# A stick-breaking attention stage: the sample pairs' value products moved behind the next pair's keys

## What is computed

```python
z = jnp.einsum('bqhd,bkhd->bhqk', qb, kb) * scale
log_beta = jnp.where(strict, jax.nn.log_sigmoid(z), NEG)
log_keep = jnp.where(strict, jax.nn.log_sigmoid(-z), 0.0)
later = lax.cumsum(log_keep, axis=3, reverse=True) - log_keep
w = jnp.exp(log_beta + later)
outs.append(jnp.einsum('bhqk,bkhd->bqhd', w, vb))
```

## Time and profile before

| | us |
|---|---|
| median of 3 runs | 1983.08 |
| lowest, highest | 1980.93, 1986.69 |
| the profiled execution | 1981.68 |
| its span | 1979.9 |
| the stage that is changed, first matmul to last copy-out | 1240.8 to 1382.2 of the span |

### The profile page before, as it was taken

How to read it: one execution, slowest core, us unless ns; L and a number is a source line. 1 busy time by engine, 2 the same in 40 slices (tenths; PEclk the granted TensorE clock), 3 DMA queues, 4 the chain that set the end, 5 groups by cost and what they waited for, 6 DMA issues and landing times.

```text
span 1979.9 us, 34330 instructions
## 1 busy us (share of the span) xinstructions
PE 1826.6 (92%) x13384; PEld 1635.6 (83%) x13384; DVE 1125.9 (57%) x2364; ACT 727.1 (37%) x1312; POOL 35.8 (2%) x65
## 2 busy tenths in 40 slices
PE   6999898989999799999999798787989999979997
PEld 5788456989999799987499796344989999979987
DVE  7973566467777642164232395675558777652263
ACT  5323345543323332245132223565553233242252
POOL 1300000000000000000000000000000000000000
PEclk9999788999999999999999857899999999989999
DMA  4134577212222232131122400864313222132211
GB/s 173 65 67 150 209 260 276 65 54 88 83 85 74 70 105 87 58 101 43 64 86 86 137 19 16 296 239 144 111 39 97 85 81 78 51 128 75 84 46 48
DMA packets 77948, 204.13 MB, mean 103 GB/s; under 512 B 12530, under 2 KB 14882, under 8 KB 77314
## 3 DMA queue, kind: packets, MB, share of 16 engines
q1 hardware_dynamic: 75762, 190.36, 28.8%
q0 software_dynamic: 2064, 12.06, 1.7%
HBM read 190.81 MB, written 10.40 MB: 102 GB/s over the span
## 4 chain that ended last, share of the span: by engine, by line
PE 79%; DVE 12%; SPq 3%; ACT 3%; issue 2%; DMA 1%; DVEq 0%; ACTq 0%
PE psum L400 42%; PE psum L573 12%; PE psum L1605 6%; PE psum L2148 3%; PE psum L408 2%; SPq L1300 1%; PE psum L832 1%; PE psum L1342 1%; PE psum L1317 1%; PE psum L495 1%; PE psum L2289 1%; PE psum L509 1%; DVE sb_arena_r L360 1%; DVE sb_ring_r L360 1%; SPq L1284 1%
## 5 line engine op out<-in xcount | busy, mean ns | idle before, releaser
L400 PE MATMUL psum<-sb_a_sb_r,sb_ring_r 128*128 128x288 f32 x1408 | 297.5, 295 | 0.0
L400 PE MATMUL psum<-sb_a_sb_r,sb_arena_r 128*128 128x288 f32 x1344 | 276.6, 296 | 0.0
L400 PE MATMUL psum<-sb_y_sb_r,sb_ring_r 128*128 128x288 f32 x960 | 263.5, 299 | 0.5 <-DVE sb_ring_r L360 0.5
L400 PEld LDWEIGHTS psum<-sb_a_sb_r,sb_ring_r 128*128 128x128 f32 x1408 | 231.3, 188 | 0.4
L400 PEld LDWEIGHTS psum<-sb_a_sb_r,sb_arena_r 128*128 128x128 f32 x1344 | 217.2, 188 | 0.0
L400 PE MATMUL psum<-sb_y_sb_r,sb_arena_r 128*128 128x288 f32 x704 | 207.2, 294 | 6.0 <-DVE sb_a_sb_r L360 5.9
L360 DVE TENSOR_TENSOR sb_ring_r<-sb_ring,sb_ring_r 128x1024 fp32r<-128x1024 f32 (+1 forms) x86 | 111.4, 1299 | 173.8 <-ACT sb_ring_r L357 172.9
L357 ACT ACTIVATE sb_ring_r<-sb_ring 128x1024 fp32r<-128x1024 f32 (+1 forms) x86 | 95.7, 1117 | 309.0 <-PE psum L400 249.1
L400 PEld LDWEIGHTS psum<-sb_y_sb_r,sb_ring_r 128*128 128x128 f32 x960 | 175.6, 190 | 1.5 <-DVE sb_ring_r L360 1.0
L573 PE MATMUL psum<-sb_arena_r 128*128 128x288 f32 x960 | 161.7, 304 | 8.2 <-DVE sb_arena_r L360 8.2
L400 PE MATMUL psum<-sb_arena_r,sb_ring_r 128*128 128x288 f32 x1056 | 145.9, 299 | 20.9 <-DVE sb_arena_r L360 20.9
(11 more groups left out here) (401 smaller groups left out, 3186.4 us busy)
## 6 DMA issues: line engine op xcount, KB each, us to landing
sb_ring<-w SPq DMA_DIRECT2D x166, 512.0 KB, 3.6
sb_ring<-wd SPq DMA_DIRECT2D x32, 704.0 KB, 4.1
sb_arena<-sb_v SPq DMA_DIRECT2D x64, 256.0 KB, 5.3
sb_arena<-moba_v SPq DMA_DIRECT2D x56, 256.0 KB, 6.6
sb_ring<-moba_k SPq DMA_DIRECT2D x32, 256.0 KB, 4.0
sb_a_sb<-moba_k SPq DMA_DIRECT2D x32, 256.0 KB, 5.5
sb_ring<-sb_k SPq DMA_DIRECT2D x32, 256.0 KB, 4.2
sb_a_sb<-sb_k SPq DMA_DIRECT2D x32, 256.0 KB, 5.2
```

Source lines behind the costliest of these rows:

```text
L400: ins = e.eng.matmul(out[:, half, :], fr(w[p][:, k, :]), fr(x[q][:, k, cols]), start=(first and k == 0 and i == 0), stop=(last and k == kb ...
```

## The change

The due lists of this stage get a third part, `final`, that holds for the last pair only. For pairs 0 to 2 the value products come behind units 12 and 13 (of the pair's own count) and the output transposes behind 16. The next pair's keys come behind unit 11. The scan keeps its place for pairs 0 to 2. For the last pair the values come behind unit 10, and log, softplus and scan one unit earlier than before.

Because the products of pair i now follow the keys of pair i+1, and both write bank 7, the waits change. In layer 1, from pair 1 on, PE waits before the keys until ACT has copied the pair before's transposed weights (`wt_ready`); the wait for its output (`y_copied`) moves from the new keys' scores to the transposes; and before its value products PE waits until DVE has read the next pair's new scores (`new_read`, a new semaphore, raised by L2662). Layer 0 keeps its due lists and waits.

```diff
         def between(pieces, u, last, due):
-            apart, units = due
+            apart, units, final = due
             for x in range(u, 8 * NPAIR + 16) if u == last else [u]:
                 for i, p in enumerate(pieces):
-                    for d in units:
+                    for d in units if i < NPAIR - 1 else final:
                         if apart * i + d == x:
                             next(p, None)
...
+            if layer == 1 and i >= 1:
+                pe.wait_ge(wt_ready, n)
             for s in range(2):
                 pe.wait_ge(kv_in[s], 16 * NPG * (n + 1))
...
                     if n >= 1:
-                        pe.wait_ge(y_copied, n)
+                        pe.wait_ge(y_copied, n if layer == 0 or i == 0 else n - 1)
...
             pe.wait_ge(sw_ready, n + 1)
+            if layer == 1 and i >= 1:
+                pe.wait_ge(y_copied, n)
             for g in range(NPG):
...
             pe.wait_ge(wt_ready, n + 1)
+            if layer == 1 and i + 1 < NPAIR:
+                pe.wait_ge(new_read, i + 2)
             for s in range(2):
...
-        DUE_A = {"pe": (8, (1, 2, 6, 7, 8, 9)), "act": (8, (5, 5, 6)), "dve": (8, (3, 4, 5, 9, 9))}
+        DUE_A = {"pe": (8, *[(1, 2, 6, 7, 8, 9)] * 2), "act": (8, *[(5, 5, 6)] * 2), "dve": (8, *[(3, 4, 5, 9, 9)] * 2)}
...
-        DUE_C = {"pe": (8, (2, 3, 9, 9, 9, 10)), "act": (8, (4, 5, 6, 8, 9)), "dve": (8, (4, 6, 7, 8, 10, 10))}
+        DUE_C = {"pe": (8, (3, 3, 10, 12, 13, 16), (3, 3, 9, 10, 10, 11)), "act": (8, (4, 6, 6, 9, 10), (4, 5, 5, 8, 9)),
+                 "dve": (8, (4, 6, 7, 8, 15, 17), (4, 5, 6, 8, 10, 11))}
...
-            do(stt(z[:, PAST:KEYS], s_new, ATT_SCALE, new, ALU.mult, ALU.add))
+            stt(z[:, PAST:KEYS], s_new, ATT_SCALE, new, ALU.mult, ALU.add).then_inc(new_read, 1)
+            v.wait_ge(new_read, i + 1)
```

More of the change, by code:

```diff
@@ L1278, in build @@
                              "rden_ready", "o_scaled", "ot_full", "y_copied"))
-        neg_ready, soft_ready, sub_ready = sem("neg_ready"), sem("soft_ready"), sem("sub_ready")
+        neg_ready, soft_ready, sub_ready, new_read = (sem(x) for x in ("neg_ready", "soft_ready", "sub_ready", "new_read"))
         def sp_stream(eng, keys, values, layer, gates):
```

## The result

The changed kernel takes 1996.29 us in the median, the kernel before 1982.31 in the same measurement. The ratio is 1.0062, with a 95% interval of 1.0049 to 1.0074: slower by 10 to 15 us. The prediction was 1995.5. The profiled execution took 1995.8 us, its span is 1994.0. The 20 executions of the changed kernel lie between 1987.4 and 2001.5 us, the 20 of the kernel before between 1978.8 and 1989.9.

What follows compares the result with a forecast made beforehand. The kernel was taken as mostly matmul-bound, this stage as a chain through PE, ACT and DVE, with key-load slack deciding. 10.2 + 2 x 2.0 = 14.2 us on 1981.7 gave 1995.9, set at 1995.5; range 1986 to 2002.

Steps and rivals of the forecast that it cites:

- Keys of pair 1: Pair 1's keys land at 1280.7 as before; PE waits some 3 us, done 1282.8 against 1287.0: 4.2 us gained.
- Units 12 and 13: Prompt matmuls of 1.71 and 2.28 us plus 4.54 of values: second value product ends at 1291.3, before 1279.5.
- SyncE's loop: Later values delay the next keys in SyncE's queue: 29.8 us in sum, pair 2's keys there at 1321.1, before 1311.7.
- PE's wait: PE stands at pair 2's keys from about 1310 and idles some 9 us; done at 1323.2 against 1319.4.
- The loop: Each later pair takes 40.4 us instead of 32 to 34; stage 10.2 us behind at pair 3's keys.
- The tail: From pair 3's keys to last copy-out, 28.9 us before: change taken as 0, bounds -0.5 to +1.5.
- The clock term: PE's clock falls at the waits for pairs 2 and 3: 2.0 us each, bounds 0 and 3.5.
- the rule of the Trainium skill: PE waiting for transfers drops to half clock, starting bursts cold: both waits at 3.5, 3 us above the sum.
- The due list by itself: Moving the 4.54 us value block off PE's way to the next keys: up to 3.8 us at three boundaries.
- A: Loads keep up, pair 2's keys landing by about 1310; 3.8 us back per boundary, about 1970; chance 0.08.
- B: Even: gain at pair 1's keys and a loop some 4 us shorter cancel the rest, 1982 to 1987; chance 0.10.
- D: Clock decides: each wait leaves PE at 1.2 GHz longer, 5 us and more per wait, 2001 to 2006; chance 0.15.

Runs made afterwards that it cites:

- the yardstick run of the same kernel: The changed kernel, unaltered, measured once more beside the run with eight extra matmuls on PE before the keys' wait: 1993.86 us, ratio 1.0058 to the kernel before.
- the one named above: Trace of the kernel before with only the last pair's own dues added; pair 0's copy came at 15.1 us; 1984.81 us, ratio 1.0008.

## Why the prediction was right

The sign and the mechanism were right, and the number lies well inside the range; that it agrees within 1 us is luck, as said below. By its own steps:

1. *Keys of pair 1.* Done at 1283.1, predicted 1282.8. PE got to the first keys later than I put it, at 1278.72 and not at 1276, and so waited 0.38 us for the second and not 3. Some 1.4 us of that are prompt matmuls at a low clock (two lines of 1.49 us from 1270.73 that take 0.81 elsewhere). It made no difference, as the landing decides.
2. *Units 12 and 13.* The second value product ends at 1291.6, predicted 1291.3.
3. *SyncE's loop.* This step carries the result. Values 8.55 us, gap 10.93, keys 14.25, landed at 1320.9; predicted 1321.1. The runs on the loads show that it is the cause: move the gap and the kernel is no slower than before (0.9974), put the keys first and every wait for a load is gone too (0.9930), lengthen the gap by 9 us in the old order and a loss appears there (1.0078), read ahead in the old order and nothing moves (0.9992).
4. *PE's wait.* 8.10 + 1.58 us, predicted about 9 apart from the first keys. PE stood there from 1307.7, predicted 1310; the first keys' matmuls, at the low clock, took up 1.7 us of the difference.
5. *The loop.* 41.9 and 41.6 us a pair, predicted 40.4 plus 2.0 for the clock.
6. *The tail.* Predicted even, at best 0.5 shorter. From pair 3's copy to the next stage it is 31.0 us against 32.0, and to the last copy-out 27.3 against 28.9, so this term was outside its bounds. Timeline of the end, after:

```profile
1392.35 0.20 PEld L2560 LDWEIGHTS psum<-sb_arena 128*64 128x64 f32 x4 [0.20 <-issue]
...
1392.49 0.42 DVE L1385 COPY sb_arena<-psum 128x256 f32<-128x256 f32 x1 [6.48 <-PE psum L1348]
1393.36 0.20 PEld L1356 LDWEIGHTS psum<-sb_con,sb_arena 128*128 128x128 f32 x2 [0.81 <-DVE sb_arena L1385]
...
1393.50 0.60 ACT L2579 ACTIVATE sb_y_sb<-psum 128x512 f32<-128x512 f32 x1 [5.16 <-PE psum L2560]
```

The prompt's last outputs (L2560) now go at 1392.35, ahead of DVE's copy, where before they stood behind the output transposes. The own dues alone, on the kernel before, shortened the same way by 0.7 us, a little more than the 0 to 0.5 that I gave them. That pair 2's values cost nothing on top, as I had it, fits these figures.

The clock term, 2.0 us a wait, measures 1.9 and 1.4 here: L1319 and L1326 take 4.00 us from 1321.04, and 3.46 at pair 3, where they took 2.07. The granted clock is 0.50 in both stretches around the waits. That each burst starts cold, the rule of the Trainium skill which the prediction cites, this trace bears out behind the waits of 8.1 us. Behind the second, short wait it does not always hold: in the yardstick run of the same kernel the second keys of pair 3 ran at a granted clock of 1.00 after a wait of 1.59 us. And paid at the full 3.5, as I read it, it was not: a good part of the stretch lies in the waiting.

The sum left one thing out. With both keys behind unit 3, pair 0's copy comes 1.5 us later (14.1 against 12.6; in the traces it is 14.1 with the new list every time and 12.6 with the old one, but for the one named above), and I had costed that move at nothing without a word. It did no harm, since pair 1 goes by the landing of its keys. The stage was predicted 14.2 us longer and is 11.9 longer: the two loops are 0.5 and 0.8 us shorter than predicted, the tail 1.0. The whole time agrees within 1 us only because 2.2 us arose outside the stage, in parts that vary by more than that from one execution to the next: in the traces here its start differs by up to 8.9 us, and what follows it by up to 5. That part of the agreement is chance. By the ratio the change costs 12.3 us, close to the stage's 11.9.

The due list by itself was sized too low. The prediction gave it up to 3.8 us at each boundary, after ACT's wait; with the keys loaded first a pair gains 5.0.

Of the rivals, A did not happen but can be had: its condition was that the keys land by about 1310. With keys loaded first those of pair 2 land at 1295.0, and the time is 1969, where A said 1970. B needed the loop 4 us shorter; D needed more from the clock than it took.

## What to carry to other kernels

When a step is moved to a later place, list what its end releases and what stands behind that in the issuing queue: here a buffer, then 16 register loads, then the keys of the pair after next. A load order and a compute order are one design. Test them together: by the ratios either half alone lost 6 or 12 us, where both gained 13 to 14.

## What the runs showed of the hardware

Page numbers read from SBUF into SyncE's registers are 0.27 us each by their record, but 16 of them with their checks hold the queue for 10.6 to 10.9 us in the loop and for 9.2 where the loop is written out; a second reading of the same numbers added 8.8 to 9.1. Right behind the value loads, 2 x 8 key loads took 17.3 to 17.5 us from first issue to last landing, against 13.9 to 14.7 with idle time ahead of them. And PE, kept busy through one wait, had a granted clock of 0.56 in the matmuls behind the next wait, 3.4 us long.
